# An expert's up matrices in units of four row blocks by 512 columns

## The chip, the cores and the metric

The kernel runs on one core of a Trainium2 chip. Its engines work side by side and meet only at semaphores: PE (TensorE, matrix products), ACT (ScalarE), DVE (VectorE), POOL (GpSimd) and SP (SyncE, which here only issues DMAs). The metric is device time in microseconds (us), the median of several runs.

## What is computed

The program is a decoder trunk of two layers on 1024 tokens of width 1024. The first layer ends in a dense SwiGLU, the second in a mixture of experts. Only the experts matter here:

```python
probs = softmax(t @ router_w + router_b)            # 8 experts
top_p, top_i = top_k(probs, 2)                      # each token goes to 2 of them
...
hid = silu(ragged_dot(xs, w1, sizes)) * ragged_dot(xs, w3, sizes)   # w1, w3: 8 x 1024 x 3584
y = ragged_dot(hid, w2, sizes) * top_p                              # w2: 8 x 3584 x 1024
```

`xs` holds the 2048 pairs of token and expert, sorted by expert. All values are float32.

## The kernel before, in words

`expert_phase` is the stage in question. A float32 product is made of three: each operand is split into a rounded part (`_hi`) and the remainder (`_lo`), and `mm3` adds hi x hi, hi x lo and lo x hi in the same bank of PSUM. So each piece of weight is loaded by SP (`raw`, a ring of 6 buffers of 1 MB), rounded by ACT (`w_hi`, 4 buffers; called the cast below), its remainder is made by DVE or POOL (`w_lo`, 4 buffers), and PE uses both.

The rows are cut into items of one expert and up to 256 rows. How many items there are, and whether an item has more than 128 rows (wide) or not (narrow), is only known on the chip: each engine loops over the items and branches. An item has 42 units of 1 MB of weights.

The first half of an item is 28 units, 7 groups of 4 (`i` and `u`). Before the change a unit is eight row blocks of 128 by 256 columns, that is, all of the inner dimension: units 0 and 1 are `w1` and `w3` for the first half of the group's 512 columns, units 2 and 3 the same for the second half. After unit 0 ACT takes the Silu of half 0 (`silu`), after unit 1 DVE multiplies it with the product of `w3` (`gated`; the semaphore `hid`) and splits the result for the second half of the item (`split`; `hid_lo`). Units 2 and 3 do the same for half 1. Wide items hold the weights still and stream 256 rows (`up`, 48 matmuls a unit, output columns by rows); narrow items hold the rows still and stream the weights (`up_unit`, 24 matmuls of 256 columns a unit), so their hidden values have to be turned by PE first (`turn_hidden`, then DVE's `turned`).

Remainders of units 0 and 2 are DVE's, those of units 1 and 3 POOL's (`rest13`). The second half of an item has 14 units of `w2` (`down`), whose remainders are all DVE's (`rest2`). Between the halves PE turns the next item's rows (`turn`, 16 transposes into the banks of the first half, so it waits for the last `hid`), ACT and DVE split them (`x_round`, `x_rest`), and PE waits in `between` for the last `hid_lo`.

The order on each engine is written out by hand. A cast of unit n waits for PE to be done with unit n-4 (`mm_done`), a load of unit n for the remainder of unit n-6.

Of the kernel before, what the change touches and what calls it, by code (L numbers as in the profile page):

```python
# [29 lines left out]
ds = bass.ds  # L30
# [1620 lines left out]
def expert_phase(nc, m, a, l):  # L1651
# [23 lines left out]
    act_t = [m.place(f"e_act{b}", [P, HALF], F32, R + (192 + 2 * b) * KB) for b in range(2)]  # L1675
    UP = 4 * NFG
# [6 lines left out]
    def by_k(t):  # L1683

        return flat(t).rearrange("p (k n) -> p k n", k=KT)
# [8 lines left out]
    with phase(nc, "x_in", "raw0", "raw1", "raw2", "raw3", "raw4", "raw5", "hi_ready", "lo1", "lo3", "lo2", "mm_done", "turned", "x_hi", "x_lo",  # L1694
               "silu", "hid", "hid_turned", "hid_hi", "hid_lo", "y_done", "y_in", "y_stored", "closed") as (block, s):
        raw_sem = (s.raw0, s.raw1, s.raw2, s.raw3, s.raw4, s.raw5)
        lo_sem = (s.lo1, s.lo3)

        @block.sync
        def _(sp):  # L1700
# [4 lines left out]
            def load13(ex, n):  # L1705
                i, u = n // 4, n % 4
                w = (a.moe_w1, a.moe_w3)[u % 2]
                sp.dma_start(by_k(raw[n % RING]),
                             w[e2, ds(ex, 1)].rearrange("o (k p) n -> p (o k) n", p=P)[:, :, P * FGRP * i + 2 * P * (u // 2):
                                                                                      P * FGRP * i + 2 * P * (u // 2) + 2 * P]  # L1710
                             ).then_inc(raw_sem[n % RING], 16)
# [6 lines left out]
            def freed(item, n):  # L1718

                if n < UP:  # L1720
                    sp.wait_ge(lo_sem[n % 2], 2 * NFG * item + 2 * (n // 4) + n % 4 // 2 + 3)
                else:
                    sp.wait_ge(s.lo2, NF2 * item + n - UP + 3)

# [29 lines left out]
        def _(act):  # L1754
# [13 lines left out]
            def silu(item, i, h, width):  # L1768
                act.wait_ge(s.mm_done, UNITS * item + 4 * i + 2 * h + 5)
                act.wait_ge(s.hid_lo, 2 * (NFG * item + i) + h + 1)  # L1770
                act.activation(act_t[h][:, 0:width], m.ps[:, h, 0:width], ACT.Silu).then_inc(s.silu, 1)

            def gate_blocks(item, width):
                for i in range(NFG - 1):
                    for h in range(2):
                        silu(item, i, h, width)
                        unit13(item, i + 1, 2 * h)
                        unit13(item, i + 1, 2 * h + 1)
                for h in range(2):
                    silu(item, NFG - 1, h, width)  # L1780
                    unit2(item, 2 * h)
                    unit2(item, 2 * h + 1)
# [5 lines left out]
            act.sem_inc(s.y_stored, 16)  # L1788
            x_round(1)
# [27 lines left out]
        def rest13(eng, item, i, u):  # L1817

            n = 4 * i + u
            eng.wait_ge(s.hi_ready, UNITS * item + n + 1)  # L1820
            eng.tensor_tensor(flat(w_lo[u]), flat(raw[n % RING]), flat(w_hi[u]).bitcast(F32), ALU.subtract).then_inc(lo_sem[u % 2], 1)  # L1821

        @block.gpsimd
        def _(pool):

            pool.sem_inc(s.lo3, 2)
# [12 lines left out]
        def _(pe):  # L1839
# [11 lines left out]

            def up(item):

                with pe.Fori(0, NFG) as i:
                    for u in range(4):
                        q, h = u % 2, u // 2
                        if u == 0:
                            pe.wait_ge(s.x_lo, item + 1)
                        if q == 0:
                            pe.wait_ge(s.hid, 2 * (NFG * item + i) + h + 1)  # L1860
                        pe.wait_ge(lo_sem[q], 2 * (NFG * item + i) + h + 3)
                        hi, lo = by_k(w_hi[u]), by_k(w_lo[u])
                        for f in range(2):
                            for k in range(KT):
                                last = mm3(pe, m.ps[:, 2 * q + h, ITEM * f:ITEM * (f + 1)], hi[:, k, P * f:P * f + P],
                                           lo[:, k, P * f:P * f + P], xg_hi[:, k, :], xg_lo[:, k, :], k == 0, k == KT - 1)
                        last.then_inc(s.mm_done, 1)

            def up_unit(item, i, u):

                q, h = u % 2, u // 2
                if u == 0:
                    pe.wait_ge(s.x_lo, item + 1)
                if q == 0:
                    pe.wait_ge(s.hid, 2 * (NFG * item + i) + h + 1)
                pe.wait_ge(lo_sem[q], 2 * (NFG * item + i) + h + 3)
                hi, lo = by_k(w_hi[u]), by_k(w_lo[u])
                for k in range(KT):
                    last = mm3(pe, m.ps[:, 2 * q + h, 0:2 * P], xg_hi[:, k, 0:P], xg_lo[:, k, 0:P], hi[:, k, :], lo[:, k, :],
                               k == 0, k == KT - 1)  # L1880
# [11 lines left out]
            def up_narrow(item):  # L1892
# [51 lines left out]
        def _(dve):  # L1944
            dve.sem_inc(s.lo1, 2)
# [10 lines left out]
            def gated(item, i, h, width):  # L1956
                g = 2 * (NFG * item + i) + h
                dve.wait_ge(s.silu, g + 1)
                dve.wait_ge(s.mm_done, UNITS * item + 4 * i + 2 * h + 6)
                dve.tensor_tensor(act_t[h][:, 0:width], act_t[h][:, 0:width], m.ps[:, 2 + h, 0:width], ALU.mult).then_inc(s.hid, 1)  # L1960
# [23 lines left out]

            x_rest(1)
# [3 lines left out]
            with dve.Fori(0, MAX_ITEMS) as item:  # L1989
                with dve.If(item < n_items):  # L1990
                    left = field(dve, item, 2, S)
                    with dve.If(left < P + 1):
                        gated(item, 0, 0, 2 * P)
                        rest13(dve, item, 1, 0)
                        gated(item, 0, 1, 2 * P)
                        turned(item, 0, 0)
                        rest13(dve, item, 1, 2)
                        for i in range(1, NFG - 1):
                            gated(item, i, 0, 2 * P)
                            turned(item, i - 1, 1)  # L2000
                            rest13(dve, item, i + 1, 0)
                            gated(item, i, 1, 2 * P)
                            turned(item, i, 0)
                            rest13(dve, item, i + 1, 2)
                        gated(item, NFG - 1, 0, 2 * P)
                        turned(item, NFG - 2, 1)
                        rest2(item, 0)
                        rest2(item, 1)
                        gated(item, NFG - 1, 1, 2 * P)
                        turned(item, NFG - 1, 0)  # L2010
                        turned(item, NFG - 1, 1)
                        rest2(item, 2)
                        rest2(item, 3)
                    with dve.Else():
                        for i in range(NFG - 1):
# [149 lines left out]
```

## Time and profile before

| what | us |
|---|---|
| median of 3 runs | 6221.68 (6217.64 to 6225.43) |
| the profiled execution: its own time | 6225.65 |
| its span, first to last instruction | 6223.8 |
| PE busy over the span | 5444.2 |
| DVE, ACT, POOL busy | 2205.8, 1831.2, 1837.4 |

The busy time of an engine is a union over its instructions, while the sum over a group of matmuls is not: matmuls overlap in the array, so 285 ns of one doesn't mean that the next starts 285 ns later. How fast PE goes is read from how many start in a window in which it is never idle. "Idle before, released by" tells what ended a wait; "issue" is a wait for which the profile has no cause. The lines of the profile are those of the kernel printed above: L253 to L255 are the three products of `mm3`, L1759 the cast of a unit of `w1` or `w3`, L1766 that of `w2`, L1771 Silu, L1807 the copy of an item's result, L1786 and L1953 the split of the next rows, L1821 the remainders of `w1` and `w3` on both engines, L1848 the turn of the next rows, L1888 the turn of the hidden values, L1960 the gating product, L1966 and L1968 its split, L1983 the remainders of `w2`.

### The profile page before, as it was taken

The numbers are of one execution on the slowest core, as the hardware profiler recorded it, in microseconds if no ns is written. First come the engines' busy times: TensorE is split into PE (matmuls) and PEld (weight loads), VectorE is DVE, ScalarE is ACT, GpSimd is POOL, SyncE is SP. The second block draws the span as 40 slices with busy tenths as digits, with TensorE's granted clock in tenths as the row PEclk, the third lists the DMA queues.
The fourth block names the chain that finished last, engine by engine and source line by source line (L and its number), as shares of the span: only waits on it lengthen the run. The fifth ranks groups of instructions, "written<-read, shape, count | busy, mean of one in ns | idle before, by whom it ended". The sixth has DMA issues, their size and how long they took to land. (4 is left out here: it accounts for less than half of the span.)

```text
span 6223.8 us, 73697 instructions
## 1 busy us (share of the span) xinstructions
PE 5444.2 (87%) x29832; PEld 4546.9 (73%) x29833; DVE 2205.8 (35%) x1993; ACT 1831.2 (29%) x1481; POOL 1837.4 (30%) x506
## 2 busy tenths in 40 slices
PE   3778879997989978887999769999999999999996
PEld 3527657775778754565776568999989998899985
DVE  8344321112202123523112223333355335753356
ACT  0113111113312121211111223333445334653344
POOL 0130111112444322120111052532534253642534
PEclk5779889998999988898999789999999999999997
DMA  9201011122333330010112065555568556985568
GB/s 387 83 0 25 17 34 46 46 86 68 91 112 98 102 104 10 14 27 22 46 46 84 19 233 193 188 189 188 195 227 276 192 182 217 332 274 182 189 223 296
DMA packets 733656, 831.56 MB, mean 134 GB/s; under 512 B 17394, under 2 KB 648306, under 8 KB 733170
## 3 DMA queue, kind: packets, MB, share of 16 engines
q1 hardware_dynamic: 724386, 794.49, 39.4%
q0 software_dynamic: 4608, 16.78, 0.8%
q10 hardware_dynamic: 4560, 18.88, 0.8%
q8 instruction: 71, 1.16, 0.1%
q14 instruction: 31, 0.25, 0.0%
HBM read 784.99 MB, written 45.09 MB: 133 GB/s over the span
## 5 line engine op out<-in xcount | busy, mean ns | idle before, releaser
L1821 POOL TENSOR_TENSOR e_w_lo<-e_raw,e_w_hi 128x2048 fp32r<-128x2048 f32 x170 | 1074.1, 6330 | 1480.8 <-ACT e_w_hi L1759 1480.8
L247 POOL TENSOR_TENSOR w_lo<-w_raw,w_hi 128x1024 fp32r<-128x1024 f32 (+1 forms) x260 | 612.4, 2357 | 2487.4 <-ACT w_hi L242 2487.4
L253 PE MATMUL banks<-h_hi,w_hi 128*128 128x512 f32 x2688 | 1086.0, 404 | 191.7 <-POOL w_lo L247 127.0
L254 PE MATMUL banks<-h_lo,w_hi 128*128 128x512 f32 x2688 | 1056.7, 393 | 0.0
L255 PE MATMUL banks<-h_hi,w_lo 128*128 128x512 f32 x2688 | 1055.8, 393 | 0.0
L253 PE MATMUL banks<-e_x_hi,e_w_hi 128*128 128x256 f32 x3584 | 1020.7, 285 | 35.1 <-issue 23.9
L254 PE MATMUL banks<-e_x_lo,e_w_hi 128*128 128x256 f32 x3584 | 1019.6, 284 | 0.0
L255 PE MATMUL banks<-e_x_hi,e_w_lo 128*128 128x256 f32 x3584 | 1019.4, 284 | 0.0
L1759 ACT ACTIVATE e_w_hi<-e_raw 128x2048 fp32r<-128x2048 f32 x340 | 648.5, 1912 | 540.2 <-PE banks L255 530.2
L253 PEld LDWEIGHTS banks<-h_hi,w_hi 128*128 128x128 f32 x2688 | 511.0, 190 | 326.8 <-issue 154.6
L253 PEld LDWEIGHTS banks<-e_x_hi,e_w_hi 128*128 128x128 f32 x3584 | 692.0, 193 | 38.3 <-issue 26.0
L254 PEld LDWEIGHTS banks<-e_x_lo,e_w_hi 128*128 128x128 f32 x3584 | 692.1, 193 | 0.0
L255 PEld LDWEIGHTS banks<-e_x_hi,e_w_lo 128*128 128x128 f32 x3584 | 691.9, 193 | 0.0
L242 ACT ACTIVATE w_hi<-w_raw 128x1024 fp32r<-128x1024 f32 (+1 forms) x260 | 272.1, 1047 | 1245.5 <-PE banks L255 981.6
L254 PEld LDWEIGHTS banks<-h_lo,w_hi 128*128 128x128 f32 x2688 | 511.6, 190 | 118.0 <-issue 14.8
L255 PEld LDWEIGHTS banks<-h_hi,w_lo 128*128 128x128 f32 x2688 | 511.0, 190 | 107.5
L1821 DVE TENSOR_TENSOR e_w_lo<-e_raw,e_w_hi 128x2048 fp32r<-128x2048 f32 x170 | 492.2, 2896 | 221.6 <-ACT e_w_hi L1759 221.6
L1983 DVE TENSOR_TENSOR e_w_lo<-e_raw,e_w_hi 128x2048 fp32r<-128x2048 f32 x168 | 390.6, 2340 | 252.1 <-ACT e_w_hi L1766 252.1
L253 PE MATMUL banks<-e_w_hi,e_hid_hi 128*128 128x512 f32 x1120 | 436.8, 390 | 0.0
L255 PE MATMUL banks<-e_w_hi,e_hid_lo 128*128 128x512 f32 x1120 | 435.9, 389 | 0.0
L254 PE MATMUL banks<-e_w_lo,e_hid_hi 128*128 128x512 f32 x1120 | 435.8, 389 | 0.0
L1766 ACT ACTIVATE e_w_hi<-e_raw 128x2048 fp32r<-128x2048 f32 x168 | 321.9, 1916 | 377.2 <-PE banks L255 377.2
(276 smaller groups left out, 6224.6 us busy)
## 6 DMA issues: line engine op xcount, KB each, us to landing
e_raw<-in_moe_w_dram SPq DMA_DIRECT2D x510, 1024.0 KB, 5.1
w_raw<-in_ffn_w_dram SPq DMA_DIRECT2D x120, 512.0 KB, 3.9
w_raw<-in_w_in_dram SPq DMA_DIRECT2D x108, 512.0 KB, 4.1
ada_w<-in_ada_w_dram SPq DMA_DIRECT2D x16, 3072.0 KB, 12.7
e_io<-row_scratch SPq DMA_DIRECT2D x13, 1024.0 KB, 6.8
y_scratch<-e_io ACTq DMA_DIRECT2D x12, 1024.0 KB, 4.2
x_res<-x_scratch SPq DMA_DIRECT2D x16, 512.0 KB, 5.8
w_br<-in_w_branch_dram SPq DMA_DIRECT2D x64, 128.0 KB, 3.9
```

The source lines that it names most:

```text
L242: act.activation(m.w_hi[b][:, 0:kt, :], m.w_raw[b][:, 0:kt, :], ACT.Copy).then_inc(s.hi_ready, 1)
L247: pool.tensor_tensor(m.w_lo[b][:, 0:kt, :], m.w_raw[b][:, 0:kt, :], m.w_hi[b][:, 0:kt, :].bitcast(F32), ALU.subtract).then_inc(s.lo_ready, 1)
L253: pe.matmul(out, wh, rh, start=first, stop=False)
L254: pe.matmul(out, wh, rl, start=False, stop=False)
L255: return pe.matmul(out, wl, rh, start=False, stop=last)
L1759: act.activation(flat(w_hi[u]), flat(raw[n % RING]), ACT.Copy).then_inc(s.hi_ready, 1)
L1766: act.activation(flat(w_hi[c % 4]), flat(raw[n % RING]), ACT.Copy).then_inc(s.hi_ready, 1)
L1821: eng.tensor_tensor(flat(w_lo[u]), flat(raw[n % RING]), flat(w_hi[u]).bitcast(F32), ALU.subtract).then_inc(lo_sem[u % 2], 1)
L1983: dve.tensor_tensor(flat(w_lo[c % 4]), flat(raw[n % RING]), flat(w_hi[c % 4]).bitcast(F32), ALU.subtract).then_inc(s.lo2, 1)
```

## The change

A unit becomes four row blocks by 512 columns: units 0 and 1 are the upper and the lower half of `w1` for all 512 columns of the group, units 2 and 3 those of `w3`. A product is complete only after its second unit. With it:

- Silu of both halves waits for unit 1, and stands on ACT behind the next group's first cast; both gating products wait for unit 3.
- In narrow items a unit is 12 matmuls of 512 columns, and the loop over the groups is written out on PE; both turns of the hidden values stand behind the next group's unit 0.
- On DVE the remainders of the next group stand ahead of a group's products; at the end of the first half three remainders of `w2` do.
- PE's unit 0 waits for both Silus of the group before, unit 2 for both products.

```diff
     def by_k(t):
 
-        return flat(t).rearrange("p (k n) -> p k n", k=KT)
+        return flat(t).rearrange("p (k n) -> p k n", k=KH)
...
+    def half_out(q, h, width):
+
+        if width == HALF:
+            return m.ps[:, 2 * q + h, :]
+        return m.ps[:, 2 * q, width * h:width * (h + 1)]
...
             def silu(item, i, h, width):
-                act.wait_ge(s.mm_done, UNITS * item + 4 * i + 2 * h + 5)
+                act.wait_ge(s.mm_done, UNITS * item + 4 * i + 6)
                 act.wait_ge(s.hid_lo, 2 * (NFG * item + i) + h + 1)
...
             def gate_blocks(item, width):
...
+                for i in range(NFG):
+                    last = i == NFG - 1
+                    for u in range(4):
+                        if last:
+                            unit2(item, u)
+                        else:
+                            unit13(item, i + 1, u)
+                        if u == 0:
+                            for h in range(2):
+                                silu(item, i, h, width)
...
+            def unit_waits(item, i, u):
+                if u == 0:
+                    pe.wait_ge(s.x_lo, item + 1)
+                    pe.wait_ge(s.silu, 2 * (NFG * item + i) + 2)
+                if u == 2:
+                    pe.wait_ge(s.hid, 2 * (NFG * item + i) + 2)
+                pe.wait_ge(rest_sem[u % 2], 2 * (NFG * item + i) + u // 2 + 3)
...
-                for k in range(KT):
-                    last = mm3(pe, m.ps[:, 2 * q + h, 0:2 * P], xg_hi[:, k, 0:P], xg_lo[:, k, 0:P], hi[:, k, :], lo[:, k, :],
-                               k == 0, k == KT - 1)
+                for k in range(KH):
+                    last = mm3(pe, m.ps[:, 2 * q, :], xg_hi[:, KH * kh + k, 0:P], xg_lo[:, KH * kh + k, 0:P], hi[:, k, :], lo[:, k, :],
+                               u % 2 == 0 and k == 0, u % 2 == 1 and k == KH - 1)
...
-                turn_hidden(item, 0, 0)
-                with pe.Fori(1, NFG) as i:
+                for i in range(1, NFG):
                     up_unit(item, i, 0)
-                    up_unit(item, i, 1)
-                    turn_hidden(item, i - 1, 1)
-                    up_unit(item, i, 2)
-                    up_unit(item, i, 3)
-                    turn_hidden(item, i, 0)
-                turn_hidden(item, NFG - 1, 1)
+                    for h in range(2):
+                        turn_hidden(item, i - 1, h)
+                    for u in range(1, 4):
+                        up_unit(item, i, u)
+                for h in range(2):
+                    turn_hidden(item, NFG - 1, h)
...
             def gated(item, i, h, width):
                 g = 2 * (NFG * item + i) + h
-                dve.wait_ge(s.silu, g + 1)
-                dve.wait_ge(s.mm_done, UNITS * item + 4 * i + 2 * h + 6)
+                dve.wait_ge(s.silu, g + 3)
+                dve.wait_ge(s.mm_done, UNITS * item + 4 * i + 8)
...
+            def next_rests(item, i):
+                if i < NFG - 1:
+                    for u in (0, 2):
+                        rest13(dve, item, i + 1, u)
+                else:
+                    for c in range(3):
+                        rest2(item, c)
...
                     with dve.If(left < P + 1):
...
+                        for u in (0, 2):
+                            rest13(dve, item, 1, u)
+                        for i in range(1, NFG):
+                            narrow_hidden(item, i - 1)
+                            next_rests(item, i)
+                        narrow_hidden(item, NFG - 1)
                     with dve.Else():
...
+                        for i in range(1, NFG):
                             for h in range(2):
-                                hidden(item, i, h)
-                                rest13(dve, item, i + 1, 2 * h)
+                                hidden(item, i - 1, h)
+                            next_rests(item, i)
                         for h in range(2):
                             hidden(item, NFG - 1, h)
-                            rest2(item, 2 * h)
-                            rest2(item, 2 * h + 1)
+                    rest2(item, 3)
                     x_rest(item + 2)
```

`narrow_hidden` is `gated` for both halves and then `turned` for both. The load of a unit reads 512 columns of four row blocks, so 2 KB in a row where it was 1 KB.

How the instructions move, first on DVE at the end of a wide item's first half, before (names with numbers are buffers; `e_act_10629` is half 0, `e_act_10630` half 1):

```order
956 L1960 TENSOR_TENSOR e_act_10629<-e_act_10629,banks 128x512
957 L1972 REGISTER_ALU
958 L1966 TENSOR_SCALAR e_hid_hi<-e_act_10629 128x512
959 L1968 TENSOR_TENSOR e_hid_lo<-e_act_10629,e_hid_hi 128x512
960 L1982 REGISTER_ALU
961 L1983 TENSOR_TENSOR e_w_lo_10625<-e_raw_10619,e_w_hi_10621 128x2048
962 L1983 TENSOR_TENSOR e_w_lo_10626<-e_raw_10620,e_w_hi_10622 128x2048
963 L1958 REGISTER_ALU
964 L1959 REGISTER_ALU
965 L1960 TENSOR_TENSOR e_act_10630<-e_act_10630,banks 128x512
```

and the same place after:

```order
958 L1993 TENSOR_TENSOR e_w_lo_10626<-e_raw_10620,e_w_hi_10622 128x2048
959 L1992 REGISTER_ALU
960 L1993 TENSOR_TENSOR e_w_lo_10627<-e_raw_10615,e_w_hi_10623 128x2048
961 L1968 ISA
962 L1969 REGISTER_ALU
963 L1970 TENSOR_TENSOR e_act_10629<-e_act_10629,banks 128x512
964 L1976 TENSOR_SCALAR e_hid_hi<-e_act_10629 128x512
965 L1977 REGISTER_ALU
966 L1978 TENSOR_TENSOR e_hid_lo<-e_act_10629,e_hid_hi 128x512
967 L1968 REGISTER_ALU
968 L1970 TENSOR_TENSOR e_act_10630<-e_act_10630,banks 128x512
```

Before, two remainders of `w2` stood between the halves' products, and the split of half 0 ahead of them; now the remainders stand first, and the second product directly behind the split of the first.

DVE in the middle of a narrow item, before:

```order
769 L1958 ISA
770 L1959 REGISTER_ALU
771 L1960 TENSOR_TENSOR e_act_10629<-e_act_10629,banks 128x256
772 L1966 TENSOR_SCALAR e_hid_hi<-banks 128x2x128
773 L1968 TENSOR_TENSOR e_hid_lo<-banks,e_hid_hi 128x2x128
774 L1820 REGISTER_ALU
775 L1821 TENSOR_TENSOR e_w_lo_10625<-e_raw_10617,e_w_hi_10621 128x2048
776 L1958 REGISTER_ALU
777 L1959 REGISTER_ALU
778 L1960 TENSOR_TENSOR e_act_10630<-e_act_10630,banks 128x256
```

and after:

```order
763 L1970 TENSOR_TENSOR e_act_10629<-e_act_10629,banks 128x256
764 L1968 REGISTER_ALU
765 L1970 TENSOR_TENSOR e_act_10630<-e_act_10630,banks 128x256
766 L1986 REGISTER_ALU
767 L1976 TENSOR_SCALAR e_hid_hi<-banks 128x2x128
768 L1978 TENSOR_TENSOR e_hid_lo<-banks,e_hid_hi 128x2x128
769 L1986 REGISTER_ALU
770 L1976 TENSOR_SCALAR e_hid_hi<-banks 128x2x128
771 L1978 TENSOR_TENSOR e_hid_lo<-banks,e_hid_hi 128x2x128
772 L1830 REGISTER_ALU
773 L1831 TENSOR_TENSOR e_w_lo_10625<-e_raw_10617,e_w_hi_10621 128x2048
774 L1830 REGISTER_ALU
```

Before, each half had its product, split and one remainder; now both products stand together, then both splits, then (the next row, not shown) both remainders. On PE, the whole program has 3835 rows before and 4001 after.

## Rows read from the trace of the kernel before

**Rows 1.** Groups of instructions from 3000 us on: wide, then narrow items' first matmuls.
```profile
L253 PE MATMUL banks<-e_x_hi,e_w_hi 128*128 128x256 f32 x3584 | 1020.7, 285 | 35.1 <-issue 23.9 <-DVE e_w_lo L1821 11.2
...
L253 PE MATMUL banks<-e_w_hi,e_x_hi 128*128 128x256 f32 x896 | 263.4, 294 | 36.2 <-POOL e_w_lo L1821 28.1 <-issue 6.1 <-DVE e_w_lo L1821 2.0
```

**Rows 2.** Timeline of ACT: start, length, line, op, times; the result copy of three items.
```profile
4364.00 1.87 ACT L1807 ACTIVATE e_io<-banks 128x2048 f32<-128x2048 f32 x1
...
4606.79 1.86 ACT L1807 ACTIVATE e_io<-banks 128x2048 f32<-128x2048 f32 x1
...
4744.76 1.86 ACT L1807 ACTIVATE e_io<-banks 128x2048 f32<-128x2048 f32 x1
```

**Rows 3.** Windows: PE, PEld, DVE, ACT, POOL busy (instructions), PE clock, DMA share, GB/s.
```profile
4710.00:4740.00 30.00, 30.00 (x134) 24.84 (x133) 23.33 (x11) 17.29 (x9) 0.00 (x0) 1.00 1.02 349
4650.00:4690.00 40.00, 37.54 (x304) 36.32 (x303) 33.32 (x25) 24.64 (x18) 40.00 (x7) 1.00 0.99 327
4150.00:4170.00 20.00, 20.00 (x169) 20.00 (x168) 5.89 (x8) 8.64 (x6) 10.14 (x2) 1.00 0.64 210
```

**Rows 4.** Timeline of DVE, then PE, at the end of a wide item's first half.
```profile
4908.35 0.69 DVE L1960 TENSOR_TENSOR e_act<-e_act,banks 128x512 f32<-128x512 f32 x1 [5.24 <-PE banks L255]
4909.07 0.43 DVE L1966 TENSOR_SCALAR e_hid_hi<-e_act 128x512 fp32r<-128x512 f32 x1
...
4910.14 4.49 DVE L1983 TENSOR_TENSOR e_w_lo<-e_raw,e_w_hi 128x2048 fp32r<-128x2048 f32 x2
...
4909.09 1.97 PE L1848 MATMUL banks<-const,e_io 128*128 128x128 f32 x16 [0.78 <-DVE e_act L1960]
```

**Rows 5.** Timeline of PE at the start of two wide items.
```profile
4121.68 0.38 PE L253 MATMUL banks<-e_x_hi,e_w_hi 128*128 128x256 f32 x1 [2.34 <-issue]
...
4995.73 0.57 PE L253 MATMUL banks<-e_x_hi,e_w_hi 128*128 128x256 f32 x1 [8.47 <-issue]
```

**Rows 6.** Timeline of PE in a narrow item's first half and at its end.
```profile
4611.61 0.38 PE L253 MATMUL banks<-e_w_hi,e_x_hi 128*128 128x256 f32 x1 [1.51 <-POOL e_w_lo L1821]
...
4624.87 0.39 PE L253 MATMUL banks<-e_w_hi,e_x_hi 128*128 128x256 f32 x1 [0.41 <-POOL e_w_lo L1821]
...
4702.59 0.43 PE L1888 MATMUL banks<-const,e_act 128*128 128x128 f32 x2 [1.41 <-DVE e_act L1960]
4702.86 1.91 PE L1848 MATMUL banks<-const,e_io 128*128 128x128 f32 x16
```

**Rows 7.** Timeline of POOL from the start of the same narrow item.
```profile
4606.96 4.59 POOL L1821 TENSOR_TENSOR e_w_lo<-e_raw,e_w_hi 128x2048 fp32r<-128x2048 f32 x1 [95.39 <-ACT e_w_hi L1759]
4613.19 5.00 POOL L1821 TENSOR_TENSOR e_w_lo<-e_raw,e_w_hi 128x2048 fp32r<-128x2048 f32 x1 [1.63 <-ACT e_w_hi L1759]
4618.49 26.23 POOL L1821 TENSOR_TENSOR e_w_lo<-e_raw,e_w_hi 128x2048 fp32r<-128x2048 f32 x4 [0.30 <-ACT e_w_hi L1759]
```

**Rows 8.** Timeline of DVE in the same narrow item.
```profile
4616.65 3.69 DVE L1821 TENSOR_TENSOR e_w_lo<-e_raw,e_w_hi 128x2048 fp32r<-128x2048 f32 x1 [1.28 <-ACT e_w_hi L1759]
4621.41 0.42 DVE L1960 TENSOR_TENSOR e_act<-e_act,banks 128x256 f32<-128x256 f32 x1 [1.07 <-PE banks L255]
4621.74 0.42 DVE L1966 TENSOR_SCALAR e_hid_hi<-banks 128x256 fp32r<-128x256 f32 x1
...
4622.54 4.42 DVE L1821 TENSOR_TENSOR e_w_lo<-e_raw,e_w_hi 128x2048 fp32r<-128x2048 f32 x1
```

**Rows 9.** Waits from 3650 to 6150 us: who for whom, total, times, longest.
```profile
ACT e_w_hi L1759 <- PE banks L255: 528.2, 163, 14.4
```

**Rows 10.** Timeline of ACT in the same narrow item and at its end.
```profile
4624.58 0.38 ACT L1771 ACTIVATE e_act<-banks 128x256 f32<-128x256 f32 x1 [1.25 <-PE banks L255]
...
4628.04 1.92 ACT L1759 ACTIVATE e_w_hi<-e_raw 128x2048 fp32r<-128x2048 f32 x1 [1.27 <-PE banks L255]
...
4704.81 1.88 ACT L1786 ACTIVATE e_x_hi<-banks 128x2048 fp32r<-128x2048 f32 x1 [1.89 <-PE banks L1848]
```

**Rows 11.** DMA queues from 4980 to 5000 us: packets, MB, share of 16 engines.
```profile
q8 instruction: 2, 0.03, 0.6%
```

More of the change, by code:

```diff
@@ L1675, in expert_phase @@
     act_t = [m.place(f"e_act{b}", [P, HALF], F32, R + (192 + 2 * b) * KB) for b in range(2)]
+    GW = P * FGRP
+    KH = KT // 2
     UP = 4 * NFG
@@ L1720, in freed @@
                 if n < UP:
-                    sp.wait_ge(lo_sem[n % 2], 2 * NFG * item + 2 * (n // 4) + n % 4 // 2 + 3)
+                    sp.wait_ge(rest_sem[n % 2], 2 * NFG * item + 2 * (n // 4) + n % 4 // 2 + 3)
                 else:
@@ L1768, in silu @@
             def silu(item, i, h, width):
-                act.wait_ge(s.mm_done, UNITS * item + 4 * i + 2 * h + 5)
+                act.wait_ge(s.mm_done, UNITS * item + 4 * i + 6)
                 act.wait_ge(s.hid_lo, 2 * (NFG * item + i) + h + 1)
-                act.activation(act_t[h][:, 0:width], m.ps[:, h, 0:width], ACT.Silu).then_inc(s.silu, 1)
+                act.activation(act_t[h][:, 0:width], half_out(0, h, width), ACT.Silu).then_inc(s.silu, 1)
             def gate_blocks(item, width):
[L1774 to L1782, printed above, removed]
+                for i in range(NFG):
[8 more added lines that the diff above has]
+                                silu(item, i, h, width)
             def x_round(count):
@@ L1788, in _ @@
             act.sem_inc(s.y_stored, 16)
+            act.sem_inc(s.silu, 2)
             x_round(1)
@@ L1855, in up @@
                     for u in range(4):
[L1856 to L1861, printed above, removed]
-                        hi, lo = by_k(w_hi[u]), by_k(w_lo[u])
-                        for f in range(2):
-                            for k in range(KT):
-                                last = mm3(pe, m.ps[:, 2 * q + h, ITEM * f:ITEM * (f + 1)], hi[:, k, P * f:P * f + P],
-                                           lo[:, k, P * f:P * f + P], xg_hi[:, k, :], xg_lo[:, k, :], k == 0, k == KT - 1)
+                        q, kh = u // 2, u % 2
@@ new lines, in up @@
+                        unit_waits(item, i, u)
+                        hi, lo = by_k(w_hi[u]), by_k(w_lo[u])
+                        for f in range(FGRP):
+                            for k in range(KH):
+                                last = mm3(pe, m.ps[:, 2 * q + f // 2, ITEM * (f % 2):ITEM * (f % 2 + 1)], hi[:, k, P * f:P * f + P],
+                                           lo[:, k, P * f:P * f + P], xg_hi[:, KH * kh + k, :], xg_lo[:, KH * kh + k, :],
+                                           u % 2 == 0 and k == 0 and f % 2 == 0, u % 2 == 1 and k == KH - 1 and f % 2 == 1)
@@ L1867, in up @@
                         last.then_inc(s.mm_done, 1)
             def up_unit(item, i, u):
[L1871 to L1876, printed above, removed]
+                q, kh = u // 2, u % 2
+                unit_waits(item, i, u)
                 hi, lo = by_k(w_hi[u]), by_k(w_lo[u])
-                for k in range(KT):
-                    last = mm3(pe, m.ps[:, 2 * q + h, 0:2 * P], xg_hi[:, k, 0:P], xg_lo[:, k, 0:P], hi[:, k, :], lo[:, k, :],
-                               k == 0, k == KT - 1)
+                for k in range(KH):
+                    last = mm3(pe, m.ps[:, 2 * q, :], xg_hi[:, KH * kh + k, 0:P], xg_lo[:, KH * kh + k, 0:P], hi[:, k, :], lo[:, k, :],
+                               u % 2 == 0 and k == 0, u % 2 == 1 and k == KH - 1)
@@ L1944, in _ @@
         def _(dve):
-            dve.sem_inc(s.lo1, 2)
+            dve.sem_inc(s.rest_dve, 2)
             dve.sem_inc(s.lo2, 2)
@@ L1983, in rest2, with narrow_hidden @@
                 dve.tensor_tensor(flat(w_lo[c % 4]), flat(raw[n % RING]), flat(w_hi[c % 4]).bitcast(F32), ALU.subtract).then_inc(s.lo2, 1)
+            def narrow_hidden(item, i):
+                for h in range(2):
+                    gated(item, i, h, 2 * P)
+                for h in range(2):
+                    turned(item, i, h)
+            def next_rests(item, i):
[5 more added lines that the diff above has]
+                        rest2(item, c)
             x_rest(1)
```

40 lines of the change are left out of this document (10 added, 30 removed).

## The prediction

> **What bounds the kernel now.** Start with the page and the list of groups: the expert stage runs from about 3617 us to 6157 us of a 6223.8 us span, and its matmuls are the largest work in the program [rows 1]. The busy columns of those groups count overlapping matmuls; the pace has to be read otherwise. The change touches nothing before 3617 us, and nothing after the stage.
>
> Next, cut the stage into items by the copy of an item's result on ACT, which stands once per item. Two of them lie 242.8 us apart for a wide item (256 rows) and 137.97 us apart for a narrow one (128 rows or fewer) [rows 2]. The list has 3584 wide triples at 448 an item, so 8 wide items, and 896 narrow ones at 224, so 4 narrow items [rows 1].
>
> Then ask, in each kind of item, which wait ends last. In the middle of a wide item PE is busy without a gap at the full granted clock, DVE is a third busy, POOL half, the DMA share is 0.64; 169 matmuls in 20 us are 0.118 us each, 5.7 us for a unit of 48 [rows 3]. Only the item's ends cost something: PE stands 0.78 us before the 16 transposes of the next rows [rows 4] and 2 to 8 us at the start of an item [rows 5].
>
> In a narrow item POOL is busy 40.00 of 40 us and PE 37.5 [rows 3]. PE starts every second unit when POOL's remainder ends, 13.26 us for two [rows 6]. Why does a POOL remainder take 6.56 us (26.23/4) there, when the lone one took 4.59 [rows 7]? DVE's remainder lasts 2.25 us alone (two in 4.49, [rows 4]), 3.69 us where POOL's previous one ended 1.54 us after it started (4613.19+5.00 = 4618.19, against 4616.65), and 4.42 in the steady state [rows 7, 8]. 1.54+2.15 = 3.69: the two engines take turns. A pair costs 4.5+2.15 = 6.65 us, as measured. So the narrow first half is set by POOL and DVE together, with PE waiting 0.41 us a time [rows 6].
>
> **Part 1: twice as many columns, half as many row blocks.** In a wide item the same 48 matmuls a unit stay, with 256 streamed columns each; cost 0. In a narrow item 24 matmuls of 256 columns become 12 of 512. The second half of a narrow item already has 512: 134 in 30 us, 0.224 us each, so 2.7 us a unit against 24 x 0.118 = 2.84 [rows 3]. That is 0.14 us saved on 28 units, 4 us an item, all of it beside POOL, which is late: worth 0 while that cover holds. The DMA rows grow from 1 to 2 KB. Nobody waits for weights: ACT's rounding waits for PE 528 us, and no row of that view over 5 us names a DMA [rows 9]. Worth 0, at most the 1 us of the stage's first load.
>
> **Part 2: the wide item's end.** A gating product may only run when all four units are done. Before, half 0 was finished early, and between the last matmul and the turn stood one product: started 4908.35, PE free at 4909.09 after 0.78 us idle [rows 4]. Now DVE does product, split high, split low, product. The product starts at 4908.35, the first split at 4909.07, and what stands behind the splits at 4910.14 [rows 4], so the second product starts 1.79 us later, and the turn with it. The three remainders that DVE now does ahead don't push it: the last needs unit 2 of the last group, then 0.3+1.9+2.3 = 4.5 us, and PE works 5.7 us on unit 3. The second product's splits (1.1 us) fit under the 1.97 us of transposes. 8 x 1.79 = +14.3 us; bounds +10 (if part of the wait is absorbed) and +18.
>
> **Part 3: the wide middle.** Silu now waits for unit 1, the product for unit 3, and PE's unit 0 and unit 2 of the next group for these. Silu has the 11.4 us of units 2 and 3, the products and splits of both halves (2 x 1.79 us) the 11.4 us of the next units 0 and 1. DVE's unit-2 remainder is ready 4.5 us after unit 2 and needed 17 us after it. Cost 0.
>
> **Part 4: the narrow middle.** Write R1, R3 for POOL's remainders, D0, D2 for DVE's, and start the clock when PE starts unit 1 of a group. It ends at 2.7, ACT reacts 0.3 later (3.17 us lie between PE's start 4624.87 and ACT's cast 4628.04, 2.84 of them matmuls [rows 6, 10]). Two Silus of 0.38 us [rows 10] now stand before the cast of unit 1, which runs 3.8 to 5.7. R1 of the next group: 5.75 to 10.25. D2 has waited since 7.7 and takes its turn: 10.25 to 12.4. Only then come both products (0.33 from start to start, 0.42 long [rows 8]), to 13.15, the second pair of transposes (0.27, from 4702.59 to the next rows' first at 4702.86 [rows 6]), and unit 1 of the next group at 13.45. The turns alone add up to 2 x 6.65 = 13.3; before it was 13.26. So a group costs +0.2 us, but it has become a closed ring PE, ACT, POOL, DVE, PE without slack.
>
> **Part 5: the narrow ends.** From the start of the item (4606.96, where R1 starts [rows 7]): R1 ends at 4.6, PE starts unit 1 at 4.64, R3 ends at 11.2 [rows 6, 7]. R3 started at 6.2, right behind its cast; ACT's next cast, of 1.9 us, ends at 8.1, and D0 of group 1 behind it waits for R3: 11.2 to 13.4. R1 of group 1 follows, to 17.9; D2, to 20.1; both products, to 20.9, transposes, and PE starts unit 1 of group 1 at 21.2. Before: 4.64+13.26 = 17.9. That is 3.3 us late, although POOL is on time; unit 3 follows without waiting at 26.6, where it was 24.5. With 5 rings of 13.45 unit 1 of the last group starts at 88.45 and unit 3 ends at 96.6; before 4.64+13 x 6.63+2.84 = 93.7. Then DVE: R3 is done at 91.9, two remainders of the second half until 96.3, the third to 98.6, products to 99.35, transposes 0.27, turn 1.95, copy of the next rows at 101.6. Before, that copy started at 4704.81-4606.96 = 97.8 [rows 10]. +3.8 us x 4 = +15 us. Bounds: 0, if POOL's pace decides as before; +8 an item (+32), if in the ring a turn slips and a group costs 1 us more.
>
> **Sum.** 14.3+15 = +29 on the profiled execution of 6225.65 us, that is 6255. The median of before is 6221.68, 4.0 less; so 6251.
>
> **Rivals.**
> (a) *Code loading.* PE's loop has 166 more rows, because the narrow path is written out where it was a loop; each matmul stands twice in the trace (weight load, matmul), so some 330 instructions more on about 1,920. In before two of the wide items started after 8.47 us of "issue" instead of 2.34, and in that window the instruction queue q8 moved two packets, in the window 4115 to 4130 around such a start with 2.34 us none [rows 5, 11]. A jump to code that isn't there costs about 6.1 us. Both cases follow a narrow and then a wide item. If each of the 4 narrow items makes one more such jump, +24 us: 6275. For it: the code grows exactly where the jumps start. Against it: straight code is loaded in time (PE is busy 30.00 of 30 us in a written-out second half [rows 3]). The Trainium skill (Runtime: NRT & Kernel Launch, Instruction fetch mechanics) gives PE an instruction memory of 128 KiB, or 2048 instructions, refilled in blocks of 256 and with a stall at a jump outside it. By that figure the loop just fits before and doesn't after; the two packets agree with it, the count of extra stalls no run here shows.
> (b) *The narrow part is free.* The ring hides in POOL's turns, at both ends too: +14 alone, 6236. For it: POOL's work is the same; against it: the late D2 in part 5.
> (c) *The ring is worse.* D2 or R1 misses its turn by a little and waits a whole one, 1.1 us a group more: +22, 6273.
> (d) *Faster.* The narrow half is paced by memory: DMA share 0.99 at 327 GB/s [rows 3], and POOL's and DVE's long times are that, not turns. With rows of 2 KB the pair would fall to PE's 2 x 2.7+0.5 = 5.9 us, 0.7 x 14 x 4 = -39, with part 2 -25: 6197. It decides from the point where DMA ends a wait. Against it: POOL took 4.59 us with DMA running, and the 3.69 us row fits turns to the hundredth.
>
> **Chances.** Forecast 0.53, (a) 0.18, (b) 0.15, (c) 0.09, (d) 0.05. A measurement of this kernel tells about 0.2% (12 us) from no change. (d) is faster, with 0.02 for what I have not seen; two thirds of (b) and a little of the forecast lie within 0.2% (6209 to 6234); the rest is slower. The range leaves out (d) and the worst of (a): 6232 to 6278.
>
> **What would show it.** In the changed profile: wide items 1.8 us longer, all in the wait before the turn (0.78 to about 2.6 us, now eight times); narrow items about 142 us; in their middle PE waits released by DVE's product where POOL's remainder stood, every 13.4 us, with unit 3 not waiting; POOL 6.6 us a remainder still. The matmuls of the narrow first half: 448 triples of 512 columns at 0.224 us. (a) would show as new "issue" gaps of 8 us at item starts or before the narrow end; (d) as POOL remainders near 5 us. I am wrong if the wait before the wide turn stays 0.8 us, or if a narrow item gets shorter.

## The result, and the profile after

The changed kernel takes 6262.32 us (median of 4, 6258.82 to 6265.52), the kernel before, beside it on the same chip, 6222.12 us. The ratio is 1.0065, 95% interval 1.0048 to 1.0082: 40 us slower. I had forecast 6251 in a range of 6232 to 6278, so the direction is right and the size is short: +29 us said, +40 measured. The profiled executions are 6262.89 and 6225.65 us, 37.2 us apart.

First cut the stage into items, as in [rows 2]. The timeline of ACT in the changed kernel shows the result copies 246.06 us apart for a wide item (before 242.8) and 142.48 for a narrow one (before 137.97):

```profile
4370.30 1.86 ACT L1817 ACTIVATE e_io<-banks 128x2048 f32<-128x2048 f32 x1
...
4616.36 1.86 ACT L1817 ACTIVATE e_io<-banks 128x2048 f32<-128x2048 f32 x1
...
4758.84 1.86 ACT L1817 ACTIVATE e_io<-banks 128x2048 f32<-128x2048 f32 x1
```

The same for all twelve, from PE's first matmul of an item to that of the next (us, in order of time; the last narrow one runs to PE's first matmul behind the stage):

| | before | after | sum |
|---|---|---|---|
| 8 wide | 244.3 244.3 242.8 242.5 250.4 245.2 250.4 245.0 | 246.8 246.1 246.1 245.7 252.2 246.2 252.2 246.0 | +16.5 |
| 4 narrow | 138.3 137.9 138.3 151.7 | 142.8 142.6 144.4 156.2 | +19.9 |

That is 36.4 of the 37.2 us. Now the end of a wide item's first half, the place of [rows 4]: DVE, then PE.

```profile
4922.32 0.69 DVE L1970 TENSOR_TENSOR e_act<-e_act,banks 128x512 f32<-128x512 f32 x1 [1.52 <-PE banks L255]
4923.04 0.43 DVE L1976 TENSOR_SCALAR e_hid_hi<-e_act 128x512 fp32r<-128x512 f32 x1
4923.50 0.69 DVE L1978 TENSOR_TENSOR e_hid_lo<-e_act,e_hid_hi 128x512 fp32r<-128x512 f32 x1
4924.11 0.68 DVE L1970 TENSOR_TENSOR e_act<-e_act,banks 128x512 f32<-128x512 f32 x1
...
4924.85 1.97 PE L1858 MATMUL banks<-const,e_io 128*128 128x128 f32 x16 [2.56 <-DVE e_act L1970]
...
5011.50 0.58 PE L253 MATMUL banks<-e_x_hi,e_w_hi 128*128 128x256 f32 x1 [8.48 <-issue]
```

The last line is the next item's first matmul, one of the two long starts that were there before [rows 5]. The second product starts at 4924.11, 1.79 us after the first, behind the first one's two splits, and PE's wait has gone from 0.78 to 2.56 us. Next a narrow item: the same waits on PE as in [rows 6].

```profile
5257.70 0.49 PE L253 MATMUL banks<-e_w_hi,e_x_hi 128*128 128x512 f32 x1 [2.03 <-issue]
...
5278.17 0.74 PE L1899 MATMUL banks<-const,e_act 128*128 128x128 f32 x4 [3.48 <-DVE e_act L1970]
5293.10 0.69 PE L1899 MATMUL banks<-const,e_act 128*128 128x128 f32 x4 [1.71 <-DVE e_act L1970]
5306.46 0.70 PE L1899 MATMUL banks<-const,e_act 128*128 128x128 f32 x4 [1.74 <-DVE e_act L1970]
5319.84 0.69 PE L1899 MATMUL banks<-const,e_act 128*128 128x128 f32 x4 [1.75 <-DVE e_act L1970]
...
5357.62 0.69 PE L1899 MATMUL banks<-const,e_act 128*128 128x128 f32 x4 [2.15 <-DVE e_act L1970]
```

In the steady part of the item PE no longer waits for POOL's remainder but for DVE's product, once a group, every 13.37 us; unit 3 does not wait. The first turn comes 20.5 us after the item's start. The rest of the ring is on POOL, DVE and ACT, to be read against [rows 7, 8, 10]:

```profile
5290.70 6.39 POOL L1831 TENSOR_TENSOR e_w_lo<-e_raw,e_w_hi 128x2048 fp32r<-128x2048 f32 x1 [0.21 <-ACT e_w_hi L1767]
5299.23 4.62 POOL L1831 TENSOR_TENSOR e_w_lo<-e_raw,e_w_hi 128x2048 fp32r<-128x2048 f32 x1 [2.13 <-ACT e_w_hi L1767]
5304.04 6.43 POOL L1831 TENSOR_TENSOR e_w_lo<-e_raw,e_w_hi 128x2048 fp32r<-128x2048 f32 x1 [0.19 <-ACT e_w_hi L1767]
...
5295.15 4.09 DVE L1831 TENSOR_TENSOR e_w_lo<-e_raw,e_w_hi 128x2048 fp32r<-128x2048 f32 x1
5301.27 4.73 DVE L1831 TENSOR_TENSOR e_w_lo<-e_raw,e_w_hi 128x2048 fp32r<-128x2048 f32 x1 [2.03 <-ACT e_w_hi L1767]
5305.92 0.74 DVE L1970 TENSOR_TENSOR e_act<-e_act,banks 128x256 f32<-128x256 f32 x2
...
5296.68 0.66 ACT L1779 ACTIVATE e_act<-banks 128x256 f32<-128x256 f32 x2 [3.34 <-PE banks L255]
5297.23 1.92 ACT L1767 ACTIVATE e_w_hi<-e_raw 128x2048 fp32r<-128x2048 f32 x1
...
5360.09 1.88 ACT L1795 ACTIVATE e_x_hi<-banks 128x2048 fp32r<-128x2048 f32 x1 [2.68 <-PE banks L1858]
```

Follow one turn: two Silus at 5296.68, the cast to 5299.15, POOL's R1 from 5299.23 to 5303.85, DVE's D2 (issued at 5301.27, waiting for its turn) to 5306.00, products, and the transposes at 5306.46. POOL is idle 2.13 us before R1, while DVE makes D0 (issued at 5295.15, done at 5299.24). POOL's two remainders now take 4.62 and 6.4 us where both took 6.6. The copy of the next rows starts 102.4 us after the item's start (before 97.8).

The waits of the stage, 3650 to 6200 us (who for whom: total, times, longest), give both as sums:

```profile
PE banks L1899 <- DVE e_act L1970: 57.3, 28, 3.5
...
PE banks L1858 <- DVE e_act L1970: 20.5, 8, 2.6
...
PE banks L253 <- POOL e_w_lo L1831: 3.7, 5, 0.9
```

POOL's part is 3.7 us where the list of groups before had 28.1 [rows 1]; that list has the 512-column matmuls now, 448 triples as forecast, in place of 896:

```profile
L253 PE MATMUL banks<-e_w_hi,e_x_hi 128*128 128x512 f32 x448 | 183.2, 409 | 11.9 <-issue 6.0 <-POOL e_w_lo L1831 3.7 <-DVE e_w_lo L1831 2.0
```

The windows (PE, PEld, DVE, ACT, POOL, clock, DMA share, GB/s), as in [rows 3], show the middle of a narrow item, the start of the third wide item, and the time just after a narrow item's first turn:

```profile
5297.00:5337.00 40.00, 34.76 (x158) 27.82 (x157) 32.90 (x25) 24.53 (x19) 33.06 (x7) 1.00 0.89 311
4124.00:4130.00 6.00, 5.31 (x32) 5.32 (x33) 1.21 (x1) 5.25 (x4) 4.58 (x1) 0.72 0.76 299
5278.00:5284.00 6.00, 5.83 (x21) 4.68 (x22) 5.66 (x7) 0.68 (x3) 4.12 (x1) 0.72 0.92 323
```

And the windows of the kernel before at the starts of its third and its fifth wide item:

```profile
4121.00:4127.00 6.00, 5.32 (x44) 5.32 (x45) 1.24 (x1) 5.25 (x4) 4.64 (x1) 1.00 0.76 284
4745.00:4751.00 6.00, 5.71 (x35) 5.72 (x36) 1.70 (x1) 5.26 (x3) 4.51 (x1) 0.72 0.92 321
```

POOL is busy 33.06 of 40 us in the middle, where it was busy 40.00. A granted clock of 0.72 over 6 us is 3.4 us of it at 1.2 GHz, the rest at 2.4. The third wide item has such a stretch at its start after the change, and had none before; the fifth had it before too.

### The profile page after: what moved, and what is told of

Its sections match the earlier page's. It is cut to its first block and busy times, and to the rows that moved or that the text cites. A ratio compares the mean times of both kernels' runs of the same rounds, so it can differ in the third digit from the quotient of the medians.

```text
span 6261.1 us, 70859 instructions
## 1 busy us (share of the span) xinstructions
PE 5437.6 (87%) x28488; PEld 4479.8 (72%) x28489; DVE 2420.2 (39%) x1993; ACT 1846.3 (29%) x1493; POOL 1598.8 (26%) x506
## 5 line engine op out<-in xcount | busy, mean ns | idle before, releaser
L1831 POOL TENSOR_TENSOR e_w_lo<-e_raw,e_w_hi 128x2048 fp32r<-128x2048 f32 x170 | 835.6, 4917 | 1754.1 <-ACT e_w_hi L1767 1754.1
L1831 DVE TENSOR_TENSOR e_w_lo<-e_raw,e_w_hi 128x2048 fp32r<-128x2048 f32 x170 | 510.9, 3005 | 758.1 <-ACT e_w_hi L1767 754.9
L1993 DVE TENSOR_TENSOR e_w_lo<-e_raw,e_w_hi 128x2048 fp32r<-128x2048 f32 x168 | 391.6, 2334 | 326.3 <-ACT e_w_hi L1774 325.6
```

What stands on the lines that cost most here:

```text
L1993: dve.tensor_tensor(flat(w_lo[c % 4]), flat(raw[n % RING]), flat(w_hi[c % 4]).bitcast(F32), ALU.subtract).then_inc(s.lo2, 1)
```

## The experiments

Each kernel was timed beside the kernel before on the same chip, and each ratio below is to that kernel. Items are read as in the table above.

**1. The wide end alone.** Both products before both splits, after the last group of a wide item.

```diff
                         for h in range(2):
-                            hidden(item, NFG - 1, h)
+                            gated(item, NFG - 1, h, HALF)
+                        for h in range(2):
+                            dve.wait_ge(s.hid, 2 * (NFG * item + NFG - 1) + h + 3)
+                            split(item, NFG - 1, h, act_t[h][:, :], ITEM)
```

> The changed kernel with one edit: at the end of a wide item's first half DVE does both gating products first and then both splits. Theory of waits: the second product starts 0.72 us behind the first instead of 1.79, so PE's wait before the rows' turn falls from 2.57 to 1.50 us, in 8 wide items: -8.6 us on the changed kernel's 6262, some 6254, ratio to before 1.0051. Rival, that the turn waits for something else (ACT or the load of the rows): the wait stays 2.57 us, 1.0065.

Measured: 6252.11 us, 1.0052 (1.0038 to 1.0066). The turn on PE, and what DVE does for it:

```profile
4915.61 1.97 PE L1858 MATMUL banks<-const,e_io 128*128 128x128 f32 x16 [1.38 <-DVE e_act L1970]
...
4914.27 1.28 DVE L1970 TENSOR_TENSOR e_act<-e_act,banks 128x512 f32<-128x512 f32 x2 [1.52 <-PE banks L255]
...
4916.99 0.69 DVE L1978 TENSOR_TENSOR e_hid_lo<-e_act,e_hid_hi 128x512 fp32r<-128x512 f32 x1
```

The wait falls by 1.19 us, as the order of DVE says. But from the turn to the item's end an item now takes 78.75 us in place of 78.16: the last split ends at 4917.68, after the 16 transposes, and the second half waits for it. Half is given back; 8 x 0.6 = 4.8 us remain. The wide items of the profile are 5.5 us shorter in all. Another 4.7 us are in the narrow items, whose code is the same: three of them are 1.5 to 1.6 us shorter. In one, the 141.0 us item from 5248.82, both stretches at 1.2 GHz are gone that the changed kernel has there (at its start and behind its first turn). The second, as a window of this run:

```profile
5268.00:5274.00 6.00, 4.73 (x23) 3.92 (x24) 5.66 (x8) 1.15 (x3) 5.27 (x1) 1.00 0.93 345
```

Its first two turns lie 13.38 us apart, where they lie 14.93 apart in the changed kernel. Why the clock stays up there isn't known. So the wait is caused by the splits in front of the second product, and the total moved further than its term.

**2. The narrow order alone.** DVE makes unit 0's remainder, both products, unit 2's remainder, then the splits; in the last group both products and splits stand before the third remainder of the second half.

```diff
-                        for i in range(1, NFG):
-                            narrow_hidden(item, i - 1)
-                            next_rests(item, i)
-                        narrow_hidden(item, NFG - 1)
+                        for i in range(NFG):
...
+                                rest13(dve, item, i + 1, 0)
...
+                            for h in range(2):
+                                gated(item, i, h, 2 * P)
+                            if i < NFG - 1:
+                                rest13(dve, item, i + 1, 2)
+                            for h in range(2):
+                                turned(item, i, h)
+                        rest2(item, 2)
```

> The changed kernel with one edit: in narrow items DVE does the next group's unit-0 remainder, both products, then the unit-2 remainder, then both splits; in the last group both products and splits stand ahead of the third remainder of w2. Theory of the closed ring: the products no longer wait for a remainder that waits for POOL; PE starts unit 1 of group 1 at 17.9 us into the item (20.5 to 21.3 now), the pace is that of POOL and DVE in turns (13.3 us a group), POOL is busy all the time again, and the narrow item goes from 142.6 us back to about 138.5: -16.6 us in all, ratio 1.0038. Rival, that the narrow items lose by the twelve 512-column matmuls or by code loading in the written-out path: nothing changes, 1.0065.

Measured: 6243.34 us, 1.0035 (1.0022 to 1.0047). Narrow items are 138.44, 138.06 and 138.48 us, those of before within 0.3. POOL is the pace again, as in [rows 3, 6]:

```profile
5276.11 0.50 PE L253 MATMUL banks<-e_w_hi,e_x_hi 128*128 128x512 f32 x1 [0.89 <-POOL e_w_lo L1831]
...
5289.35 0.50 PE L253 MATMUL banks<-e_w_hi,e_x_hi 128*128 128x512 f32 x1 [0.87 <-POOL e_w_lo L1831]
```

The window over its middle:

```profile
5292.00:5332.00 40.00, 36.09 (x159) 28.29 (x158) 36.63 (x24) 24.68 (x18) 40.00 (x7) 1.00 0.95 334
```

13.24 us a group, POOL 40.00 of 40. So the whole narrow term comes from what DVE does ahead of the products: D2 in the groups, and the third remainder of `w2` in the last one. This run moves both; of the 4.4 us that an item gains, 3.6 are already there at the first turn (16.84 us into the item, where it was 20.5).

**3. Both orders**, the two edits together.

> Both edits of DVE's order together. If the two terms are separate they add up: -25 us on 6262, 6237, ratio 1.0024; what is then left over before is 8 x 0.72 us of the wide turn and some short stretches of half clock. If one hides the other: less than the sum.

Measured: 6235.48 us, 1.0021 (1.0012 to 1.0030). Wide items as in 1, narrow ones as in 2: the terms add. Its wide items are 9.2 us longer in all than before, its narrow ones 0.7.

**4. Rows of 1 KB.** The changed kernel with each 1 MB weight piece fetched by two DMAs, which have rows of 1 KB in the first half.

```diff
+                for c in range(2):
+                    cols = slice(GW * i + 2 * P * c, GW * i + 2 * P * (c + 1))
+                    sp.dma_start(by_k(raw[n % RING])[:, :, 2 * P * c:2 * P * (c + 1)],
...
```

> The changed kernel with each 1 MB load issued as two DMAs, those of w1 and w3 with rows of 1 KB as before the change, those of w2 with rows of 4 KB each as now. Theory: nobody waits for weights, so 0 (ratio 1.0065, up to 1.007 for the doubled issues). Rival, that the 2 KB rows gain something that hid a larger loss elsewhere: slower by 4 us an item or more, 1.009 and up.

Measured: 6260.80 us, 1.0068 (1.0054 to 1.0082), items equal to those of the changed kernel within 0.2 us. The size of the rows, with twice as many DMAs, is worth nothing there.

**5. Three of four remainders on DVE**, on top of 3, in narrow items only: DVE also makes unit 1's, and POOL, which waits for it, passes the count on with an operation of 0.2 us.

```diff
                                 rest13(dve, item, i + 1, 0)
+                                rest13(dve, item, i + 1, 1, s.rest_more)
...
+                            pool.wait_ge(s.rest_more, (NFG - 1) * item + i)
+                            pool.tensor_tensor(told[:, :], m.const[:, K_EPS:K_EPS + 1], m.const[:, K_EPS:K_EPS + 1],
+                                               ALU.subtract).then_inc(s.rest_pool, 1)
+                            rest13(pool, item, i, 3)
```

> Both edits of DVE's order, and in narrow items DVE also makes the remainder of unit 1, so that POOL has one of four (POOL does a one-column subtraction to pass the news on). Turns of POOL and DVE then cost 4.5+3 x 2.2 = 11.1 us a group, PE needs 4 x 2.7+0.7 = 11.5. Theory (narrow pace is the turns): groups at about 11.6 us instead of 13.4, a narrow item some 131 us, -30 us against the kernel with both edits: 6207, ratio 0.9976, faster than before. Rival (narrow pace is memory, at 311 to 327 GB/s): the pace stays over 13 us, ratio 1.002 or more.

Measured: 6198.56 us, 0.9965 (0.9953 to 0.9977), narrow items 129.24, 128.92 and 129.18 us. A window over the middle of one, and PE's turns:

```profile
4640.00:4680.00 40.00, 39.92 (x181) 32.06 (x180) 39.79 (x32) 27.63 (x21) 22.14 (x8) 1.00 1.01 361
```

```profile
4643.81 0.60 PE L1908 MATMUL banks<-const,e_act 128*128 128x128 f32 x4
4655.54 0.60 PE L1908 MATMUL banks<-const,e_act 128*128 128x128 f32 x4
...
4701.51 0.69 PE L1908 MATMUL banks<-const,e_act 128*128 128x128 f32 x4 [1.74 <-DVE e_act L1979]
```

A group falls to 11.73 us, with PE busy 39.92 of 40, DVE 39.79 and the DMA at 361 GB/s; which of PE and DVE sets that pace isn't settled. So the 327 GB/s of [rows 3] was no limit, which refutes rival (d).

**6. The same with rows of 1 KB** (the edit of 4 on 5).

> The same with rows of 1 KB for w1 and w3 (each load as two DMAs). Once POOL does not set the pace a narrow group takes 4 MB in 11.6 us, 362 GB/s, and before the change 1 KB rows were seen at 327 to 349 GB/s at a full DMA share, the 2 KB rows at 382. Theory: here the wider rows matter, ACT waits for DMA in narrow items, +1 to +8 us against the run with 2 KB rows a narrow item, ratio 0.998 to 1.003. Rival: the row size is worth nothing, same time as with 2 KB rows.

Measured: 6198.47 us, 0.9964 (0.9950 to 0.9977), narrow items 129.25, 128.93 and 129.20. I had expected the small rows to cost something at that pace; they cost no time. A window over the middle of a narrow item shows the DMA share at 1.10, where it was 1.01 in 5:

```profile
4634.00:4674.00 40.00, 39.96 (x181) 32.03 (x180) 39.80 (x32) 27.60 (x21) 21.54 (x8) 1.00 1.10 348
```

The 382 GB/s of the expectation is no figure for rows of 2 KB: where the changed kernel has that rate, from 5358 to 5364 us, its 599 packets carry 2.29 MB, so they are the 4 KB ones of `w2`.

**7. Code size: the kernel before, with PE's narrow loop written out**, and nothing else. PE's loop over the items, counted in the built program with each matmul twice, grows from about 1,930 instructions to about 2,950; the changed kernel has about 2,270.

```diff
-                with pe.Fori(1, NFG) as i:
+                for i in range(1, NFG):
```

> The kernel before with PE's loop over a narrow item's groups written out, nothing else: some 480 matmuls more of code. Code-loading rival: each narrow item or the item behind it gets a stall of 6.1 us more, +24 us, ratio 1.004. Mine: loading of straight code is hidden, the two long starts stay two, 1.000.

Measured: 6245.14 us, 1.0038 (1.0025 to 1.0052): 24 us, and my expectation was wrong. PE's first matmuls of items:

```profile
4751.68 0.58 PE L253 MATMUL banks<-e_x_hi,e_w_hi 128*128 128x256 f32 x1 [8.37 <-issue]
5002.29 0.57 PE L253 MATMUL banks<-e_x_hi,e_w_hi 128*128 128x256 f32 x1 [8.36 <-issue]
...
5393.65 0.57 PE L253 MATMUL banks<-e_w_hi,e_x_hi 128*128 128x256 f32 x1 [10.41 <-DVE e_w_lo L1821]
...
5537.52 0.58 PE L253 MATMUL banks<-e_x_hi,e_w_hi 128*128 128x256 f32 x1 [10.69 <-issue]
```

The line of the instruction queue from 3660 to 6150 us (packets, MB, share):

```profile
q8 instruction: 54, 0.88, 0.1%
```

The start at 5002.29 was long before too (and one more, not shown). The three after narrow items took 2.0 to 2.4 us and now take 8.4 to 10.7, and q8 moved 54 packets against 24 before. Five long starts against two are three more (the expectation of 9 says four). The mechanism of rival (a) exists. The changed kernel has no more of it than the kernel before: 25 packets, and the same two long starts.

**8. The kernel before with three remainders on DVE** in narrow items (the edit of 5 on the old units).

> The kernel before (units of eight row blocks by 256 columns) with the remainder of a narrow item's unit 1 on DVE too, as in the run with three on DVE. The turns no longer set the pace, PE does: 4 x 2.84+1.0 = 12.4 us a group against the changed form's 11.5. Theory: a narrow item some 132 to 134 us against 129.0 of the changed form, so that the 512-column matmuls are worth 3 to 5 us an item once POOL's cover is gone; wide items as before; total some 6198 to 6204, ratio 0.996 to 0.997. Rival, that a matmul of 512 columns is worth nothing there: 129 us an item, 6184, ratio 0.994.

Measured: 6216.63 us, 0.9995 (0.9986 to 1.0004): no change, where I had expected a gain. Its narrow items take 138.1, 137.8 and 136.6 us. DVE, then PE, in the first of them, and the window over its middle:

```profile
4619.01 6.60 DVE L1822 TENSOR_TENSOR e_w_lo<-e_raw,e_w_hi 128x2048 fp32r<-128x2048 f32 x1
...
4625.66 0.38 PE L253 MATMUL banks<-e_w_hi,e_x_hi 128*128 128x256 f32 x1 [2.66 <-DVE e_w_lo L1822]
...
4689.80 0.39 PE L253 MATMUL banks<-e_w_hi,e_x_hi 128*128 128x256 f32 x1 [2.66 <-DVE e_w_lo L1822]
```

```profile
4640.00:4680.00 40.00, 40.00 (x337) 40.00 (x336) 33.48 (x30) 27.53 (x21) 20.83 (x7) 1.00 1.07 350
```

From the start to the next rows' transposes it takes 95.8 us, the kernel of 5 takes 86.8. PE's waits in that stretch are 7.8 us against 2.6. That is 5.2 of the 9.0 us. Behind each wait of 2.66 us PE runs at a lower granted clock in this item (0.72 from 4690 to 4696 us too); behind the first one of the third narrow item, which starts at 5372.08, it does not:

```profile
4626.00:4632.00 6.00, 6.00 (x40) 6.00 (x39) 5.09 (x4) 1.60 (x2) 0.20 (x1) 0.72 0.89 286
...
5397.00:5403.00 6.00, 6.00 (x53) 6.00 (x52) 5.38 (x6) 3.77 (x3) 0.19 (x1) 1.00 1.06 350
```

That item is 1.5 us shorter to the same point (94.3), so the two stretches are some 3.0 us. About 0.8 us are left, and a group in the middle takes 11.95 us against 11.73. So it is mostly DVE's order, with its waits and the low clock behind them, that eats the gain, and not the longer matmuls; other orders of DVE on the old units were not tried.

**9. PE's narrow groups in a loop again**, on 3: the six groups behind the first in a loop, with one wait (`y_in`) moved a unit earlier; PE's loop over the items is then about 1,740 instructions.

```diff
                     up_unit(item, 0, u)
-                pe.wait_ge(s.y_in, item + 1)
-                for i in range(1, NFG):
+                    if u == 2:
+                        pe.wait_ge(s.y_in, item + 1)
+                with pe.Fori(1, NFG) as i:
```

> The changed kernel with both edits of DVE's order and with PE's groups of a narrow item in a loop again, so that PE's loop over items is 1,737 instructions (2,268 written out, 1,928 before the change, 2,941 in the run with the old form written out, which had four stalls more). Theory that a jump outside what is loaded stalls PE: the two starts of 8.4 us fall to 2.3, -12 us on 6235, ratio 1.0002. Rival, that they have another cause than the size of the code: still 8.4 us, 1.0021.

Measured: 6222.62 us, 1.0002 (0.9993 to 1.0011), 12 us from experiment 3 (6235.48). The two long starts are gone, in the timeline of PE:

```profile
4998.16 0.38 PE L253 MATMUL banks<-e_x_hi,e_w_hi 128*128 128x256 f32 x1 [2.31 <-issue]
...
5765.39 0.38 PE L253 MATMUL banks<-e_x_hi,e_w_hi 128*128 128x256 f32 x1 [2.29 <-issue]
```

q8 moves 2 packets in the same stretch as above. With 7, the effect of the loop's code is shown from both sides: more of it brings long starts, less of it removes them. Whether its length decides or the places of its branches is not separated; about 1,930 and about 2,270 instructions give the same two.

**10. All that paid**: 5 and 9 together, the new units with both orders, three remainders on DVE and the loop.

> The same with three remainders on DVE in narrow items. If the code's size causes the two long starts: -12 us on 6198.5, 6186, ratio 0.9946; if not, 0.9965.

Measured: 6182.47 us, 0.9942 (0.9928 to 0.9955): 38 us faster than the kernel before and the fastest of all. Narrow items 129.2, 128.9 and 129.2 us, no long start.

## Why the prediction was right in direction and short in size

- **Part 1** (shape worth 0 under POOL's cover) and the rows (0): right. Experiments 4 and 6 show the rows at nothing; in experiment 2, POOL as busy as before, the new shape gains nothing. Where POOL no longer covers it, a group takes 11.73 us with it (5) and 11.95 without (8): 0.22 us, less than half of the 4 x 0.14 of part 1, with DVE without a gap in 5.
- **Part 2** (+1.79 us a wide item, 14.3 in all): right to the hundredth; the wait went to 2.56 us, eight times, 20.5 us in the list of waits.
- **Part 3** (wide middle 0): the mechanism right, but the wide items lengthened by 16.5, not 14.3. The first half takes 165.6 us in the five items that are neither the first nor start long. Before, these five took 162.3 (twice) or 163.8 (three times), and the 163.8 are those with 3.4 us at 1.2 GHz at the start: 1.5 us more. After, 162.3+1.79+1.49 = 165.58, and all five have a granted clock of 0.72 in a window of 6 us at their start. I had no term for it. Why the granted clock falls there oftener (PE stands 2.3 us in front in both) stays open.
- **Part 4** (a closed ring of 13.45 us, PE, ACT, POOL, DVE, PE): right; measured 13.37. The detail "POOL 6.6 us a remainder still" was wrong for R1, though part 4's own walk had it right (5.75 to 10.25): it starts when D0 is done and has no turn to wait for, so it takes 4.6. R1, D2, R3 and D0 follow each other without a gap, 4.6+2.15+4.5+2.15 = 13.4 us. So the turns fill the ring, and a middle group is only 0.1 us longer than before (13.26); the loss is at the item's ends.
- **Part 5** (+3.8 us a narrow item): the step that was undersized. The first new turn is at 20.5 us, its end at 21.2, as said. The next comes 14.93 us later (5278.17 to 5293.10), not 13.45: the clock is 0.72 there, and in the item of experiment 1 where it is 1.00 the two lie 13.38 apart. Then four rings of 13.37 and the last at 102.4, not 101.6. Measured 4.5 to 4.7 us in three items and 6.2 in one with more such time: 19.9 for my 15.
- **Sum**: 29.3 expected, 36.4 in the items; 2.2 of the 7 missing are in the wide items, 4.9 in the narrow ones, and the low clock carries most of both. With both orders undone (3) the narrow items are at +0.7 us, so nothing of their 19.9 is left unexplained; the wide ones keep +9.2, and the remaining wait and the late last split make 8 x (0.6+0.6) = 9.6 by sum, so the stretches at the low clock about cancel in that run.
- **Rivals**: (a) did not happen in this change, though 7 and 9 show that its mechanism is real here. (b) and (c) are refuted by the items; (d) by 4 and 5. My reason against (a), that straight code is loaded in time, doesn't speak against it: 7 is straight code too, and has three long starts more, each at a jump behind a narrow item. Why about 2,270 instructions bring none more than about 1,930 stays open; that (a) didn't happen here was luck in part.

## What to carry to other kernels

When a unit is made larger, look at what each engine must finish before the next engine may start, and put the short operations that release it ahead of the rest: the order of DVE's operations alone was worth 0.44% here (1.0065 to 1.0021). A remainder moved off the engine that sets the pace pays only if the rest of the order lets it: here moving one of four to DVE was worth another 0.56% with the new order (1.0021 to 0.9965), and 0.05% on the kernel before (8). Count the instructions of the loop body before writing a loop out, and time both forms.

## What the runs showed of the hardware

- POOL and DVE take turns on the same kind of subtraction: 4.6 us alone on POOL and 2.3 on DVE. Where two meet, the second's record holds its wait too: 6.4 to 6.6 us on POOL and 3.7 to 4.7 on DVE in the rows shown. Giving DVE three of four remainders is therefore faster (11.73 us a group) than two and two (13.24).
- A start that must load code costs 6 us (8.4 against 2.3), or 8 (10.4 to 10.7), with packets on q8. Two such starts at about 1,930 and at about 2,270 instructions, five at about 2,950, none at about 1,740. The Trainium skill (Runtime: NRT & Kernel Launch, Instruction fetch mechanics) gives 2048 instructions for PE; by that figure the loop of about 1,930 fits, and the trace doesn't agree: it has two long starts. The section puts the stall at a branch out of "the current 2-page window", with 256 instructions in a block, which is narrower than the prediction has it; the trace of 9 doesn't agree with that either, with a loop of about 1,740 and no long start.
- Weights in rows of 1 or 2 KB give the same time, also at a group of 11.7 us (5 and 6). The DMA share is higher with rows of 1 KB, 1.10 against 1.01.
